# Attention stage of a two-block network: the pooling branch goes first, first scores move into the projection, the mask goes to TensorE

## The reference, cut to what matters

```python
proj = h @ w_in                                   # 512 x 1024 @ 1024 x 2048
q, k, v, u = jnp.split(proj, [512, 1024, 1536], axis=-1)
q = rmsnorm_2(q.reshape(b, s, 4, 2, 64), qk_g[0]) # 4 heads, two maps of 64 each
k = rmsnorm_2(k.reshape(b, s, 4, 2, 64), qk_g[1])
lam = exp(sum(lq1 * lk1)) - exp(sum(lq2 * lk2)) + lam_init
# per head and block of 128 queries, for both maps:
sc = einsum('bhqd,bhkd->bhqk', q, k) * 64 ** -0.5
sc = where(kpos <= qpos, sc, -inf);  w = softmax(sc_1) - lam * softmax(sc_2)
o = rmsnorm_2(w @ v, subln_g) * (1 - lam_init)
# pooling: window means over 2, 4, 8, 16 tokens less u, then @ pool_w, * pool_scale
return concatenate([o, p], axis=-1) @ w_out       # 512 x 1024 @ 1024 x 1024
```

## Time and profile before

| | |
|---|---|
| median of three runs | 2880.39 us (2879.53 to 2882.75) |
| the profiled execution | 2878.74 us, of which the span is 2876.6 us |
| busy in the span | PE 96%, PEld 78%, DVE 50%, ACT 32%, POOL 1% |
| granted TensorE clock, mean over the span | 0.978 |
| projection with w_in | 1355.5 to 1452.8 us |
| tiles, to the start of w_out's product | 1454.0 to 1534.1 us |

### The profile page before, as it was taken

One profiled execution on the slowest core, in us unless ns is written; L12 is line 12 of the kernel. 1 busy time (PEld: TensorE's weight loads), 2 busy tenths in 40 slices (PEclk: granted clock), 3 DMA queues, 4 the chain that ended last, 5 costly groups with the idle time before them and its releaser, 6 DMA issues.

```text
span 2876.6 us, 32115 instructions
## 1 busy us (share of the span) xinstructions
PE 2747.4 (96%) x12573; PEld 2255.2 (78%) x12573; DVE 1435.5 (50%) x1561; ACT 929.1 (32%) x1087; POOL 29.0 (1%) x50
## 2 busy tenths in 40 slices
PE   7999999999999699999968999999999999999998
PEld 6888878778777488887846788887888878788887
DVE  6677553488889733325264433344333454533333
ACT  4555423332222332224343322134222332332221
POOL 0000000000000000000030000000000000000000
PEclk9999999999999899999979999999999999999999
DMA  4111222377778233232311232322323222233322
GB/s 133 60 58 59 66 88 85 97 281 278 289 297 303 85 102 95 95 99 77 100 38 44 88 102 88 102 88 88 102 88 103 88 93 97 75 104 99 102 88 73
DMA packets 252092, 323.43 MB, mean 112 GB/s; under 512 B 5622, under 2 KB 242420, under 8 KB 243828
## 3 DMA queue, kind: packets, MB, share of 16 engines
q1 hardware_dynamic: 240740, 245.51, 26.6%
q10 hardware_dynamic: 11280, 76.94, 6.8%
HBM read 320.34 MB, written 2.10 MB: 112 GB/s over the span
## 4 chain that ended last, share of the span: by engine, by line
PE 84%; DVE 10%; issue 2%; ACT 2%; DMA 1%; ACTq 0%; SPq 0%; DVEq 0%
PE po L622 22%; PE po L624 21%; PE po L623 21%; PE po L596 3%; PE po L601 3%; PE po L597 3%; DVE w_lo L1379 2%; DVE ada_acc L1732 2%; PE pm L742 2%; PE po L705 1%; PE po L707 1%; PE po L706 1%; DVE ada_tr L1741 1%; PE pm L655 1%; DMA ada_in<-in_w_ada_dram 1%
## 5 line engine op out<-in xcount | busy, mean ns | idle before, releaser
L1379 DVE TENSOR_TENSOR w_lo<-w_raw,w_hi 128x1024 fp32r<-128x1024 f32 x472 | 561.9, 1220 | 503.2 <-ACT w_hi L970 503.1
L970 ACT ACTIVATE w_hi<-w_raw 128x1024 fp32r<-128x1024 f32 x472 | 479.1, 1051 | 900.1 <-PE po L624 871.5
L622 PE MATMUL po<-a_hi,w_hi 128*128 128x512 f32 x1792 | 700.7, 391 | 4.1 <-DVE w_lo L1379 4.1
L624 PE MATMUL po<-a_hi,w_lo 128*128 128x512 f32 x1792 | 698.4, 390 | 0.0
L623 PE MATMUL po<-a_lo,w_hi 128*128 128x512 f32 x1792 | 698.3, 390 | 0.0
L622 PE MATMUL po<-b_hi,w_hi 128*128 128x512 f32 x1152 | 457.2, 397 | 16.8 <-DVE b_lo L1768 15.1
L624 PE MATMUL po<-b_hi,w_lo 128*128 128x512 f32 x1152 | 453.8, 394 | 0.0
L623 PE MATMUL po<-b_lo,w_hi 128*128 128x512 f32 x1152 | 451.1, 392 | 0.0
L622 PEld LDWEIGHTS po<-a_hi,w_hi 128*128 128x128 f32 x1792 | 337.1, 188 | 75.5 <-DVE w_lo L1379 4.9
L623 PEld LDWEIGHTS po<-a_lo,w_hi 128*128 128x128 f32 x1792 | 337.2, 188 | 70.7 <-issue 0.7
L624 PEld LDWEIGHTS po<-a_hi,w_lo 128*128 128x128 f32 x1792 | 337.1, 188 | 70.6
(11 more groups left out here) (251 smaller groups left out, 2469.5 us busy)
## 6 DMA issues: line engine op xcount, KB each, us to landing
ada_in<-in_w_ada_dram ACTq DMA_DIRECT2D x64, 1152.0 KB, 5.7
w_raw<-in_ffn_wg_dram SPq DMA_DIRECT2D x44, 1024.0 KB, 5.3
w_raw<-in_ffn_wu_dram SPq DMA_DIRECT2D x44, 1024.0 KB, 5.3
w_raw<-in_w_ff_dram SPq DMA_DIRECT2D x32, 1024.0 KB, 5.3
w_raw<-in_ffn_wd_dram SPq DMA_DIRECT2D x32, 1024.0 KB, 5.1
w_raw<-in_w_in_dram SPq DMA_DIRECT2D x28, 1024.0 KB, 5.1
w_raw<-in_ffn_wd_dram SPq DMA_DIRECT2D x16, 768.0 KB, 4.7
w_raw<-in_w_in_c_dram SPq DMA_DIRECT2D x12, 1024.0 KB, 5.1
```

Source lines behind the costliest of these rows:

```text
L622: pe.matmul(o, wh, hi[:, k, :], start=(k == ks[0]), stop=False)
L624: mm = pe.matmul(o, wl, hi[:, k, :], start=False, stop=(k == ks[-1]))
L970: act.activation(w_hi[:, s, part], w_raw[:, s, part], ACT.Copy).then_inc(hi_done, 1)
L1379: dve.tensor_tensor(w_lo[:, s, part], w_raw[:, s, part], w_hi[:, s, part].bitcast(F32), ALU.subtract).then_inc(lo_done, 1)
```

## The change

The u panels are loaded and projected first (units 0 and 1), then q and k (2 to 5), then v (6, 7). GpSimd starts its window sums as soon as both u units are read out, and uses `pr` instead of `ev` as its work space. All four pooled products stand inside and behind the first v unit, each in its own bank of `pm`, and their scaling and splitting follow at once. The scores of tile 0 stand in the middle of the second v unit; ScalarE makes tile 0's exps before it reads that unit out. w_hi and w_lo of w_out's first two units stand ahead of the rounds. Lambda is computed ahead of the q and k units.

The mask is added by TensorE: `ident_r` and `causal_r` are float32r copies made at the start of the stage, and behind each score product comes `ident_r` x `causal_r`, added to the diagonal block in the same bank. The factor 0.125 goes into the gain of q; the maximum is written negated by the reduction itself; lambda is a second factor in the scaling of map 2.

```diff
+        ident_r = sb("ident_r", [P, P], F32R, cursor[0])
+        causal_r = sb("causal_r", [P, P], F32R, cursor[0] + 4 * P)
...
-            square(w_in_ab_2[0], U_AB, 8)
+            wab = view(w_in_ab_2[0])
+            for k in range(2):
+                load(k, 2 * (U_AB + k) - 2, wab[:, :, (6 + k) * PAN:(7 + k) * PAN])
+            with sp.Fori(1, 4) as i:
+                for k in range(2):
+                    load(k, at(i, 4, 2 * (U_AB + k) - 2), wab[:, :, ds(i * 2 * PAN + (k * PAN - 2 * PAN), PAN)])
...
-                    dst = ev[:, 0, (m % 2) * S:(m % 2 + 1) * S]
+                    dst = pr[:, 0, m % 2, :]
...
                 for r in range(2):
-                    mm = pe.matmul(pm[:, 2 * (n % 2) + r, 0:(i + 1) * P],
-                                   qk[64 * r:64 * r + 64, h, i * P:(i + 1) * P],
-                                   qk[64 * r:64 * r + 64, 4 + h, 0:(i + 1) * P], start=True, stop=True)
+                    b = 2 * (n % 2) + r
+                    pe.matmul(pm[:, b, 0:(i + 1) * P], qk[64 * r:64 * r + 64, h, i * P:(i + 1) * P],
+                              qk[64 * r:64 * r + 64, 4 + h, 0:(i + 1) * P], start=True, stop=False)
+                    mm = pe.matmul(pm[:, b, i * P:(i + 1) * P], ident_r[:, :], causal_r[:, :], start=False, stop=True)
                 mm.then_inc(s_a_pe, at_pe.one(f"s{h}{i}"))
...
             def pooled(g):
                 pe.wait_ge(s_win, win_pool.after(f"pf{g}"))
-                pe.matmul(pm[:, g % 2, :], pool_m[:, g, :], pu[:, g, :], start=True, stop=True)\
+                pe.wait_ge(s_a_act, at_act.after(f"ln{2 + g // 2}"))
+                pe.matmul(pm[:, g, :], pool_m[:, g, :], pu[:, g, :], start=True, stop=True)\
...
+            def sums_and_pooled():
+                pe.wait_ge(at_landed, 5 * 16)
+                head_sum(3)
+                pooled(0)
+                pooled(1)
+
+            def first_scores():
+                pe.wait_ge(s_a_dve, at_dve.after("py1"))
+                taken(pe, U_AB + 4)
+                taken(pe, U_AB + 5)
+                scores(0)
+
+            for v in range(2):
+                product(v, U_AB + v, DK, a_hi, a_lo, normed("01") if v == 0 else None,
+                        wait_hi=normed_hi("01") if v == 0 else None)
+            for v in range(4):
+                product(v % 2, U_AB + 2 + v, DK, a_hi, a_lo, between=(lambda: head_sum(v - 1)) if v >= 1 else None)
+            product_tokens(0, U_AB + 6, between=sums_and_pooled)
+            pooled(2)
+            pooled(3)
+            product_tokens(1, U_AB + 7, between=first_scores)
+            pe.wait_ge(s_a_dve, at_dve.after("py3"))
             scores(1)
...
+            tokens_taken(0)
+            for g in range(4):
+                pooled_hi(g)
             exps(0)
+            tokens_taken(1)
...
-                dve.tensor_tensor(sc2[:, :, i * P:N], sc2[:, :, i * P:N],
-                                  causal[:, :].unsqueeze(1).to_broadcast([P, 2, P]), ALU.add)\
-                    .then_inc(s_a_dve, at_dve.one(f"mk{h}{i}"))
-                dve.wait_ge(s_a_dve, at_dve.after(f"mk{h}{i}"))
-                dve.tensor_reduce(nb, sc2, AX.X, ALU.max).then_inc(s_a_dve, at_dve.one(f"mx{h}{i}"))
-                dve.wait_ge(s_a_dve, at_dve.after(f"mx{h}{i}"))
-                dve.tensor_scalar(nb, nb, -0.125, None, ALU.mult).then_inc(s_a_dve, at_dve.one(f"nb{h}{i}"))
+                dve.tensor_reduce(nb, sc2, AX.X, ALU.max, negate=True).then_inc(s_a_dve, at_dve.one(f"mx{h}{i}"))
...
-                dve.tensor_tensor(sm[:, 1:2], sm[:, 1:2], small[:, 4:5], ALU.mult)\
-                    .then_inc(s_a_dve, at_dve.one(f"rl{h}{i}"))
...
+                dve.tensor_scalar(pr[:, n % 2, 1, 0:N], pr[:, n % 2, 1, 0:N], sm[:, 1:2], small[:, 4:5],
+                                  ALU.mult, ALU.mult).then_inc(s_a_dve, at_dve.one(f"p{h}{i}"))
...
+            pooled_scaled(0)
+            pooled_scaled(1)
+            pooled_lo(0)
+            pooled_lo(1)
+            pooled_scaled(2)
+            pooled_scaled(3)
+            weight_lo(U_ABO, s=0)
+            pooled_lo(2)
+            pooled_lo(3)
             maxima(0)
             maxima(1)
+            weight_lo(U_ABO + 1, s=1)
```

More of the change, by code:

```diff
@@ L900, in _ @@
                     scores(k + 2)
-                if k == len(TILES) - 1:
-                    pe.wait_ge(s_a_act, at_act.after(f"e1{tile[k - 1]}"))
-                    pooled(0)
-                    pooled(1)
                 if k < len(TILES):
@@ L927, in _ @@
                         mm.then_inc(s_a_pe, at_pe.one(f"ss{h}"))
-                if k == len(TILES):
-                    for g in (2, 3):
-                        pe.wait_ge(s_a_dve, at_dve.after(f"py{g - 2}"))
-                        pooled(g)
             down(U_ABO, DK, lambda k: pe.wait_ge(s_a_dve, at_dve.after(f"pl{k - 4}" if k >= 4 else f"yl{k}")),
@@ L1275, in _ @@
                 act.dma_start(lam_in[:, m, :], v.to_broadcast([P, 64])).then_inc(at_landed, 16)
+            act.activation(ident_r[:, :], ident[:, :], ACT.Copy).then_inc(s_a_act, at_act.one("ir"))
+            act.activation(causal_r[:, :], causal[:, :], ACT.Copy).then_inc(s_a_act, at_act.one("cr"))
+            for v in range(2):
+                done(U_AB + v)
+                act.activation(pu[:, 2 * v:2 * v + 2, :].rearrange("p b n -> p (b n)"),
+                               po[:, v, :, :].rearrange("p b n -> p (b n)"), ACT.Copy).then_inc(out_taken[v], 2)
+                weight_hi(U_AB + 2 + v, s=v)
+                if v == 0:
+                    act.wait_ge(s_a_dve, at_dve.after("l1"))
+                    act.activation(small[:, 2:4], small[:, 2:4], ACT.Exp).then_inc(s_a_act, at_act.one("lam"))
             for v in range(4):
-                done(U_AB + v)
+                done(U_AB + 2 + v)
                 act.activation(ev[:, v % 2, :], po[:, v % 2, :, :].rearrange("p b n -> p (b n)"), ACT.Square)\
@@ L1286, in _, with tokens_taken @@
                     .then_inc(s_a_act, at_act.one(f"rs{v}"))
-                weight_hi(U_AB + v + 2, s=v % 2)
-            for v in range(2):
-                done(U_AB + 4 + v)
+                weight_hi(U_AB + v + 4, s=v % 2)
+            def tokens_taken(v):
+                done(U_AB + 6 + v)
                 act.activation(vv[:, :, v * PAN:(v + 1) * PAN],
@@ L1292, in _ @@
                     .then_inc(out_taken[v], 2)
-                weight_hi(U_AB + 6 + v, s=v)
-            for v in range(2):
-                done(U_AB + 6 + v)
-                act.activation(pu[:, 2 * v:2 * v + 2, :].rearrange("p b n -> p (b n)"),
-                               po[:, v, :, :].rearrange("p b n -> p (b n)"), ACT.Copy).then_inc(out_taken[v], 2)
                 weight_hi(U_ABO + v, s=v)
-            act.wait_ge(s_a_dve, at_dve.after("l1"))
-            act.activation(small[:, 2:4], small[:, 2:4], ACT.Exp).then_inc(s_a_act, at_act.one("lam"))
             def exps(n):
@@ L1860, in _ @@
                         .then_inc(out_taken[s], 1)
[L1861 to L1870 removed]
+                weight_lo(U_AB + v + 4, s=s)
             def maxima(n):
```

94 lines of the change are left out of this document (24 added, 70 removed).

## The result

| | before | after |
|---|---|---|
| median of the runs, us | 2880.39 (2879.53 to 2882.75) | 2892.49 (2890.25 to 2894.65) |
| span of the profiled execution, us | 2876.6 | 2890.7 |
| mean granted TensorE clock | 0.978 | 0.972 |

The ratio is 1.004, 95% interval 1.0027 to 1.0053: 12.1 us slower where 10.5 faster was forecast. 2892.5 lies outside the range of 2860 to 2881 and next to the rival of 2894 that had a chance of 0.06.

What follows compares the result with a forecast made beforehand. Attention: no engine full, a ring of waits over TensorE, ScalarE and VectorE; elsewhere TensorE bounds. Projection +4.9, opening -9.9, heads -1.1, end -6.7 make -12.8; with 2.3 allowed for a clock fall, -10.5: 2870 us, range 2860 to 2881.

Steps and rivals of the forecast that it cites:

- the one on the clock: Later attention heads: fuller TensorE might stay at 2.4 GHz instead of falling to 1.2, giving back 2.1 us per head.
- the piece before them: Attention between the opening and the first full tile (8.6 us): no VectorE cut, +2.2 - 1.1 = +1.1 us.
- rival 3: Clock stays at its lower level through all heads while scores run one after the other: +13.7 us, 2894; chance 0.06.
- The price of the series: Heads: a mask between the two score products makes them run one after the other; +2.2 us per head.
- one fall in the forecast: Attention: allowance of 2.3 us for about one clock fall left, where four happened before; turns -12.8 into -10.5.
- Rival 1: Score halves still overlap despite the mask between them, in heads and opening: -18 us, 2862; chance 0.13.
- The projection: Before attention, TensorE full: pooled products 3.4, first tile's scores with mask 1.1, panels held 0.4; +4.9 us.
- rival 4: Projection: GpSimd holds VectorE's w_lo under every key and query panel and TensorE waits; -7 us, 2873; chance 0.11.
- The opening: Last projection matmul to tile 3's transposes: steps removed and GpSimd gone from beside VectorE, 23.5 to 13.6 us, -9.9.
- The VectorE steps: Heads: mask, negation and lambda product leave VectorE, -1.5 us per head; a scaling losing its faster rate would cost 0.4.
- The end: Tile 15's scores to w_out's first product: 16.8 to 10.1 us, pooled halves ready early, no stop; -6.7 us.
- the signs that I named: Full-tile scores near 2.4 us, not overlapping; opening 13 to 16 us; head 15.4 us, clock near 1.00; w_out without a stop.

Runs made afterwards that it cites:

- the two variants that differ in rows alone: Changed kernel, score-mask-score-mask order kept: score products over all 128 rows, 2866.97 us; scores and masks over the lower 64 rows, 2885.74 us.
- 64-row variant: Changed kernel, score-mask-score-mask order kept, with both score and both mask products over the lower 64 rows alone: 2885.74 us, ratio 1.0015 to the kernel before.
- paired kernel: Changed kernel with only the order different, both score products first and both mask products behind them: 2868.15 us, ratio 0.9957 to the kernel before.

## Why the prediction was wrong

- **The step that failed** is the one on the clock: "Against it stands the clock ... If the clock stays at 2.4 GHz, 2.1 us come back per head". I took a busier TensorE for one at a higher clock. The prediction gave back 2.1 us in each of the two heads and 1.1 in the piece before them for a clock that stays up. It did not stay up: its mean was 0.50 to 0.71. What made it busier were 64-row products in series, and with those the clock stayed low for 72 us; the two variants that differ in rows alone put about 18.8 us on it. The remark against rival 3, that in every head before the clock came back once TensorE was busy for some microseconds, was true of heads whose score products ran side by side, and was carried over to heads where they don't.
- **The price of the series** was right. I had 2.4 us for a full tile and doubled it for the lower clock; it was 2.50 and 4.65. Each change of rows cost 0.18 on average, I had 0.15. The rule of the Trainium skill that I set against the trace (TensorEngine Tiling (Array Packing), Key Properties: a change of the tiling mode drains TensorE) is borne out for the sum: the row that I read against it, transposes at 1501.11 beside a pass recorded to 1501.18, did not mean that every change is free. The change in that very place, ahead of the transposes, is cheap by the rows of the 64-row variant too (0.07 us at the lower clock); it is the changes between score and mask that cost.
- **Rival 3** had the mechanism right, and the total (2894 for 2892.5) with some luck, since its errors cancel. Its opening was too kind (-7.5, was -5.0), its heads were uneven (+6 twice, were +3.0 and +7.9) and its end too dear (-3.3, was -5.6). I gave it 0.06 and allowed 2.3 us for one fall in the forecast. No rival but the third priced the clock staying down for longer, and the range ended before it.
- **Rival 1** (the halves overlap in spite of the mask) did not happen in this order: the first map's passes were recorded to 1511.74 (1510.65 + 1.09), the second's began at 1511.93.
- **The projection**: +4.7 within the stage for +4.9. GpSimd's window sums lay under the panels; rival 4 did not happen. The other 1.3 us arose before this stage, within the scatter named above.
- **The opening** (-9.9, was -5.0): VectorE's part held. In the paired kernel it ended the weights of tile 3 12.8 us after the last projection matmul, where I had worked out 13.6; TensorE, at its lower clock there, came to their transposes after 14.3. In the changed kernel TensorE took its place, with the scores of tile 3 alone at 4.7 us.
- **The VectorE steps** went as described and no scaling lost its rate, but two factors cost 0.06 us more per 512 columns than one.
- **The end**: w_out's first product ran without a stop, -5.6 for -6.7, at a mean clock of 0.60. The -6.7 counts the stop of 0.57 that came behind the landmark used here; from w_out's first product to the end of the span the two kernels took 1342.5 and 1342.3 us, so only 0.2 of it shows there.
- My forecast of -10.5 is near what the paired kernel measured (-11.0), and that is luck. Its heads of 15.8 and 14.4 average 15.1, where I had 15.4, but mine carried 2.2 for the series and took 2.1 off for a clock that stays up, and the paired kernel has neither.
- Of the signs that I named, the scores near 2.4 us in pairs that don't overlap came true, and so did the sign of being wrong, a clock that stays near 0.8 or below.

## What to carry to other kernels

Before a pass is put between two products that each fill half of the array, ask whether they were running side by side: price the loss of that overlap, the change of rows on both sides, and then the same sum at the lower clock, and give the low case a real chance. A TensorE that is busy by time is not thereby at its full clock; look at how much of the array its passes fill. Where a pass over all rows must be added to such a pair, put it behind the pair and not between its two products.

## What the runs showed of the hardware

- The same passes in the same order were at the lower clock for 78 us with 64 rows and, by the mean of 0.89 over 63 us, for 14 with 128 (17 with the part that ran on into w_out's product).
- Useless 128-row passes made a kernel faster: two on each of 14 tiles brought the attention of the paired kernel from 64.7 to 59.4 us.
- Adding a 2 x 128-column mask by two products behind the pair took 0.28 us at the full clock; VectorE's step took 0.43. In a kernel that had already lost its other VectorE steps, the choice made no difference that the runs can tell (2868.2 and 2865.4, with intervals that overlap).
